# Four accumulating bias scatters moved behind the next gather, and the overflow branch moved ahead of the last rows, in a hybrid mixer and mixture-of-experts kernel

## The chip, the core and the metric

The kernel runs on one core of a Trainium2 chip. The metric is device time in microseconds (us). A lower number is better. The engines are named as the profile names them: PE (TensorE matmul), PEld (its weight load), DVE (VectorE), ACT (ScalarE), POOL (GpSimd) and SP (SyncE). A "q" behind a name (POOLq, SPq) marks work that the engine's sequencer does alone: semaphore waits, register loads, branches, drains.

## What is computed

512 tokens of width 1024 go through a normalisation, two attention-like mixers, a second normalisation and then a mixture of 32 experts of which each token takes four. The last part is where the change lies:

```python
def moe_ffn(h, w_router, b_router, w_gate_up, b_gate_up, w_down, b_down):
    logits = (xt @ w_router + b_router).astype(jnp.float32)
    top_val, top_idx = lax.top_k(logits, TOP_K)
    gates = jax.nn.softmax(top_val, axis=-1)
    ...
    def expert_block(args):
        xb, e = args
        gu = xb @ w_gate_up[e] + b_gate_up[e]
        gate = jnp.minimum(gu[:, :D_FF], SWIGLU_LIMIT)
        up = jnp.clip(gu[:, D_FF:], -SWIGLU_LIMIT, SWIGLU_LIMIT)
        glu = gate * jax.nn.sigmoid(SWIGLU_ALPHA * gate)
        return ((up + 1.0) * glu) @ w_down[e] + b_down[e]
    ys = lax.map(expert_block, (xs, blk_e)).reshape(P, D)
    ys = ys * slot_g[:, None].astype(ys.dtype)
    out = jax.ops.segment_sum(ys, slot_tok, num_segments=T)
...
h = layer_norm(DEEPNORM_ALPHA * h + ffn, ln_ffn_g[l], ln_ffn_b[l])
```

## The kernel before

Every float32 product is made of three passes over split numbers (a high and a low part, L1536 to L1538). For each weight tile ACT makes the high part (L901, `whi<-raw`), DVE subtracts it to get the low part (L1301, `wlo<-raw,whi`), and PE uses both. SP loads the tiles, 1 MB each, twelve for an expert: eight for gate and up, four for down. Six raw slots and four split slots go round; SP may load a tile as soon as DVE has split the tile six places earlier (`after`, L474).

**A step.** All five engines run a loop over i, one expert in a step. In step i PE multiplies the eight gate and up tiles of expert i, adds the bias (L1896, raises `gu_done`), transposes the gathered rows of the next expert (`turn_x`, L1543 from `xg`), multiplies the four down tiles of expert i-1, and transposes the activated rows (`turn_a`, L1543 from `act_t`). DVE splits tiles 4 to 8 of the step (counted from 0), then waits until the results of expert i-2 have been added in memory (`y_out`, ahead of L1435), copies the next row lists into `didx` and `gidx` (L1435 to L1439, raises `tab_ready`), splits tiles 9 to 11, which are the last three down tiles, and goes on to the clamps (L1377, L1379) and to the product that makes `act_t` (L1385).

**GpSimd's order.** POOL issues its DMAs in the order of the code, and a wait in it holds all that is written behind. A step of its loop (`body`, L667) is: wait for `gu_done` of this step; two small loads of the next bias (L643); the gather of rows for the expert after the next (L627), which needs `tab_ready` and the transpose `turn_x` of the rows before; then the scatter of the finished rows (`scatter`, L638), which adds `y_t` into `acc_dram` and needs ACT's `y_t` (L965) and the landing of the scatter before.

**The bias of the down product.** The gated sum of `b_down` is made once for all tokens in step 2, on PE and ACT, and lies in the tile `h2`. Four DMAs (L680), 512 KB each, add it to `acc_dram`, one for each 128 tokens, with the row numbers in `ridx`. All accumulating DMAs on `acc_dram` may not overlap those on the same rows, so the four wait for the scatter before them (`y_out`), and the next scatter waits for them (`bias_added`). The kernel before issues them behind body 2 and waits for them there, ahead of step 3 with its gather.

**The end.** After the results of 31 experts have been added, SP loads `acc_dram` in four parts, DVE normalises them, and SP stores them (`finish`, L508, L511). The rows of the last expert go another way: POOL gathers them from `acc_dram` (L691), DVE adds and normalises (L1492 to L1499, raises `last_ready`), and POOL writes them over the stored output (L697, `last_out`). An expert can have more than 128 rows; further blocks are in an overflow branch, entered if `count` (read from `ovtab`) is above zero. In these inputs it is not entered. Before, POOL takes that branch (L699) behind L697, and SP reads `count` (L519) and branches (L520) after it has waited for `last_out`. Behind its last work each engine drains and joins a barrier (L2017).

Of the kernel before, what the change touches and what calls it, by code (L numbers as in the profile page):

```python
# [13 lines left out]
ALU = mybir.AluOpType  # L14
ACT = mybir.ActivationFunctionType
F32 = mybir.dt.float32
# [8 lines left out]
T = 512  # L25
TT = T // P
# [7 lines left out]
E = 32  # L34
# [80 lines left out]
def build(nc, a, out):  # L115
    base = -(-nc.sbuf_base // 128) * 128
# [44 lines left out]
    bias_raw = at("bias_raw", 176, [P, 512])  # L161
    bias_hi = at("bias_hi", 179, [P, 512], F32R)
    bias_lo = at("bias_lo", 182, [P, 512], F32R)
# [130 lines left out]
    raw_in = [S(f"raw_in{s}") for s in range(XRAW)]  # L294
    hi_ready, lo_ready = S("hi_ready"), S("lo_ready")
    small_hi, small_lo = S("small_hi"), S("small_lo")
    bias_hi_s, bias_lo_s, bias_out = S("bias_hi_s"), S("bias_lo_s"), S("bias_out")
    h_norm, h_turned, hT_hi_s, hT_lo_s, h_out, h_back = (
        S("h_norm"), S("h_turned"), S("hT_hi_s"), S("hT_lo_s"), S("h_out"), S("h_back"))
    half_done = S("half_done")  # L300
# [41 lines left out]
    acc_in = [S(f"acc_in{t}") for t in range(TT)]  # L342
    acc_out, last_in, last_ready, last_out = S("acc_out"), S("last_in"), S("last_ready"), S("last_out")
    fin_ready, fin_out, over_done = S("fin_ready"), S("fin_out"), S("over_done")
    dve_seq, act_seq, fin_seq = S("dve_seq"), S("act_seq"), S("fin_seq")
    afin_seq = S("afin_seq")
    var_ready, std_ready, gsqrt_done = S("var_ready"), S("std_ready"), S("gsqrt_done")
# [82 lines left out]
    @block.sync  # L430
    def _(sp):
        def load_x(t):
            sp.dma_start(xt[:, t, :], x_tiles[t]).then_inc(x_in[t], 16)

        def load_params():
            w_in = a["w_in"][0].rearrange("(k p) c -> p k c", p=P)
            sp.dma_start(sm_raw[:, :, 0:RANK], w_in[:, :, C_LOW:C_LOW + RANK]).then_inc(small_in, 16)
            sp.dma_start(sm_raw[:, :, RANK:RANK + FH], w_in[:, :, C_FF:C_FF + FH]).then_inc(small_in, 16)
            sp.wait_ge(w_up_zero, 1)
            sp.dma_start(w_up[0:RANK, :], a["w_gla_gate_up"][0]).then_inc(params_in, 16)  # L440
            sp.dma_start(w_up[32:33, :], a["b_gla_gate"]).then_inc(params_in, 16)
            sp.dma_start(b_f, bcast(a["b_forget"][0], FH)).then_inc(params_in, 16)
            with nc.allow_non_contiguous_dma(reason="256 gains onto partitions"):
                sp.dma_start(g_norm, a["g_gla_norm"][0].rearrange("(c p) -> p c", p=P)).then_inc(params_in, 16)
            sp.dma_start(w_rt[:], a["w_router"][0].rearrange("(k p) e -> p k e", p=P)).then_inc(params_in, 16)
            sp.dma_start(b_rt[:], bcast(a["b_router"][0], E)).then_inc(params_in, 16)
            sp.dma_start(bias_raw[:], a["b_gate_up"][0].rearrange("e (q c) -> (e q) c", c=512)).then_inc(bias_in, 16)

        load_x(0)
        load_x(1)  # L450
        sources = {n: a[n][0] for n in ("w_in", "w_gla_proj", "w_fox_proj", "w_out")}
        for c, (kind, j, source, col) in enumerate(DENSE):
            if c >= RAW:
                o = c - RAW
                sp.wait_ge(hi_ready, o + 1)
                sp.wait_ge(lo_ready, o + 1)
            src = sources[source].rearrange("(k p) c -> p k c", p=P)[:, :, col:col + CW]
            sp.dma_start(raw[:, c % RAW, :].rearrange("p (k c) -> p k c", k=KT), src).then_inc(raw_in[c % RAW], 16)
            if c == 0:
                load_x(2)  # L460
                load_x(3)
            if c == RAW - 1:
                load_params()

        def load_gu(e, c, slot):
            sp.dma_start(xraw(slot), w_gu[e, c * P:(c + 1) * P, :]).then_inc(raw_in[slot], 16)

        def load_dn(e, q, slot):
            src = w_dn[e, 2 * q * P:2 * (q + 1) * P, :].rearrange("(p k) c -> p k c", k=2)
            sp.dma_start(xraw(slot).rearrange("p (k c) -> p k c", k=2), src).then_inc(raw_in[slot], 16)  # L470

        def after(n):

            sp.wait_ge(lo_ready, NCD + n + 1)  # L474


        sp.wait_ge(half_done, 2 * (NPROJ + 4))
        for c in range(2):
            sp.dma_start(pre[:, c, :], w_gu[0, c * P:(c + 1) * P, :]).then_inc(pre_in[c], 16)
        sp.wait_ge(wo_done, 2 * TT - 1)  # L480
        load_gu(0, 6, 0)
        load_gu(0, 7, 1)
        sp.wait_ge(wo_done, 2 * TT)
        load_gu(0, 2, 2)
        load_gu(0, 3, 3)
        sp.wait_ge(lg_done, TT)
        load_gu(0, 4, 4)
        load_gu(0, 5, 5)

        def body(i):  # L490

            for c in range(STEPC):
                after(tile_no(i, c) - XRAW)
                if c < GUC:
                    load_gu(i, c, tile_slot(c))
                else:
                    load_dn(i - 1, c - GUC, tile_slot(c))

        with sp.Fori(1, E) as i:
            body(i)  # L500
        for q in range(DNC):
            after(tile_no(E, q) - XRAW)
            load_dn(E - 1, q, tile_slot(q))

        def finish(n):

            for t in range(TT):
                sp.dma_start(acc[:, t, :], acc_tiles[t]).then_inc(acc_in[t], 16)  # L508
            for t in range(TT):
                sp.wait_ge(fin_ready, TT * n + t + 1)  # L510
                sp.dma_start(out_tiles[t], acc[:, t, :]).then_inc(fin_out, 16)  # L511
            sp.wait_ge(fin_out, 16 * TT * (n + 1))

        sp.wait_ge(y_out, 16 * (E - 1))
        finish(0)

        sp.wait_ge(last_out, 16)
        sp.wait_ge(routed, 1)
        count = sp.value_load(ovtab[0:1, 2 * OVMAX:2 * OVMAX + 1], min_val=0, max_val=OVMAX)  # L519
        with sp.If(count > 0):  # L520
            with sp.Fori(0, count) as j:
                e = sp.value_load(ovtab[0:1, bass.ds(j, 1)], min_val=0, max_val=E - 1)
                for c in range(STEPC):
                    after(NMAIN + STEPC * j + c - XRAW)
                    if c < GUC:
                        load_gu(e, c, c % XRAW)
                    else:
                        load_dn(e, c - GUC, c % XRAW)
            sp.wait_ge(over_done, 1)
            finish(1)  # L530


    @block.gpsimd
    def _(pool):
# [44 lines left out]
            pool.wait_ge(h_norm, t + 1)  # L579
            g.dma_start(h_tiles[t], xt[:, t, :]).then_inc(h_out, 16)  # L580

        pool.wait_ge(bias_hi_s, 1)
        pool.wait_ge(bias_lo_s, 1)
        for s, part in enumerate((bias_hi, bias_lo)):
            g.dma_start(bgu_dram[s].rearrange("(p c) -> p c", p=P), part[:]).then_inc(bias_out, 16)

# [77 lines left out]
        g.dma_start(lnffn_g[:], bcast(a["ln_ffn_g"][0])).then_inc(lnffn_in, 16)  # L664
        g.dma_start(lnffn_b[:], bcast(a["ln_ffn_b"][0])).then_inc(lnffn_in, 16)

        def body(i, last):  # L667
            if not last:
                pool.wait_ge(gu_done, i + 1)
                load_bgu(i + 1)  # L670
                gather(i + 3, i + 2)
            scatter(i - 1)

        body(1, False)
        body(2, False)
        pool.wait_ge(y_out, 16 * 2)
        pool.wait_ge(ridx_ready, 1)
        for t in range(TT):
            pool.wait_ge(stage_ready, TT + t + 1)
            g.indirect_dma_start(acc_dram, bass.IndirectOffsetOnAxis(ap=ridx[:, t:t + 1], axis=0), h2[:, t, :], None,  # L680
                                 bounds_check=token_bound, oob_is_err=False, compute_op=ALU.add).then_inc(bias_added, 16)
        pool.wait_ge(bias_added, 16 * TT)
        with pool.Fori(3, E - 1) as i:
            body(i, False)
        body(E - 1, True)

# [4 lines left out]
        g.indirect_dma_start(xg[:], None, acc_dram, bass.IndirectOffsetOnAxis(ap=didx[:, 0:1], axis=0),  # L691
                             bounds_check=token_bound, oob_is_err=False).then_inc(last_in, 16)
        count = pool.value_load(ovtab[0:1, 2 * OVMAX:2 * OVMAX + 1], min_val=0, max_val=OVMAX)
        pool.wait_ge(last_ready, 1)
        pool.wait_ge(fin_out, 16 * TT)
        pool.sem_inc(scatters, 1)
        g.indirect_dma_start(out[0], bass.IndirectOffsetOnAxis(ap=didx[:, 0:1], axis=0), up_t[:], None,  # L697
                             bounds_check=token_bound, oob_is_err=False).then_inc(last_out, 16)
        with pool.If(count > 0):  # L699
            pool.wait_ge(last_out, 16)  # L700
            scatter(E - 1)
            with pool.Fori(0, count) as j:
                e = pool.value_load(ovtab[0:1, bass.ds(j, 1)], min_val=0, max_val=E - 1)
                gather(E + 4 + j, E + 1 + j)
                load_bgu(e)
                scatter(E + j)


    @block.scalar
    def _(act):  # L710
# [49 lines left out]
        act.wait_ge(small_in, 32)  # L760
        s_.copy(sm_hi[:], sm_raw[:]).then_inc(small_hi, 1)
        act.wait_ge(bias_in, 16)
        s_.copy(bias_hi[:], bias_raw[:]).then_inc(bias_hi_s, 1)

        def evacuate(c, half):

# [278 lines left out]
    def _(dve):  # L1045
# [49 lines left out]
        h_lo(3)  # L1095
        dve.wait_ge(small_hi, 1)
        v.tensor_tensor(sm_lo[:], sm_raw[:], sm_hi[:].bitcast(F32), ALU.subtract).then_inc(small_lo, 1)
        dve.wait_ge(bias_hi_s, 1)
        v.tensor_tensor(bias_lo[:], bias_raw[:], bias_hi[:].bitcast(F32), ALU.subtract).then_inc(bias_lo_s, 1)

        def hook(s):
            if s == 5:
# [937 lines left out]
```

## Time and profile before

| quantity | value |
|---|---|
| median of 3 runs | 1833.65 us (1832.83 to 1834.01) |
| the profiled execution | 1832.18 us |
| its span | 1830.6 us |
| granted TensorE clock, mean | 0.987 of full speed |
| PE busy | 1765.0 us, 96% of the span |
| DVE busy | 1360.5 us, 74% |
| ACT busy | 1096.5 us, 60% |
| POOL busy | 305.3 us, 17% |
| read from HBM | 476.12 MB |

The span is the part of the profiled execution between its first and last instruction; 1.58 us lie around it. A stretch in which PE follows matmul on matmul is set by PE. Where PE waits, the row says in square brackets how long and for whom, and from there one goes back: to the engine that came late, to what that engine waited for, until an instruction is reached that nothing held. The trace's chain of work does the same from the end of the program.

### The profile page before, as it was taken

How to read it: one execution, taken by the hardware profiler on the slowest of the kernel's cores; microseconds unless marked ns; L12 is line 12 of the kernel's file. 1: busy time of each engine (PE TensorE's matmuls, PEld its weight loads, DVE VectorE, ACT ScalarE, POOL GpSimd, SP SyncE). 2: the span in 40 equal slices, each digit the busy share in tenths (PEclk: the TensorE clock that was granted, in tenths of full speed). 3: DMA queues.
4: the chain of work that ended last, by engine and by line, in shares of the span. 5: the costliest groups of instructions: out<-in, count | busy, mean ns of one | idle time of the engine just before them, and what ended most of it. 6: DMA issues, size and time to landing. Idle time of an engine off the chain costs nothing.

```text
span 1830.6 us, 24973 instructions
## 1 busy us (share of the span) xinstructions
PE 1765.0 (96%) x9025; PEld 1470.8 (80%) x9026; DVE 1360.5 (74%) x1180; ACT 1096.5 (60%) x895; POOL 305.3 (17%) x222
## 2 busy tenths in 40 slices
PE   6999999999999999999999999999999999999992
PEld 6897798888888977777888888888888888888882
DVE  6314533433346689979999999999999999999995
ACT  3522323455413257767777877777777777787772
POOL 3000000000000056231212122121221221212211
PEclk9999999999999999999999999999999999999996
DMA  7322123122233289999999999999999999999973
GB/s 255 109 75 70 47 70 92 47 70 70 92 113 138 84 328 335 379 369 379 366 368 388 364 367 389 372 367 382 377 371 379 385 367 369 391 368 367 387 301 109
DMA packets 122621, 487.51 MB, mean 266 GB/s; under 512 B 18822, under 2 KB 63878, under 8 KB 73418
## 3 DMA queue, kind: packets, MB, share of 16 engines
q1 hardware_dynamic: 106642, 455.66, 64.7%
q0 software_dynamic: 15920, 31.12, 6.1%
q8 instruction: 37, 0.61, 0.1%
q14 instruction: 14, 0.11, 0.0%
q10 hardware_dynamic: 8, 0.01, 0.0%
HBM read 476.12 MB, written 27.84 MB: 275 GB/s over the span
## 4 chain that ended last, share of the span: by engine, by line
PE 88%; DVE 4%; DMA 3%; issue 1%; ACT 1%; POOL 0%; POOLq 0%; ACTq 0%; DVEq 0%
PE psA L1536 21%; PE psA L1538 20%; PE psA L1537 20%; PE psX L1538 6%; PE psX L1537 6%; PE psX L1536 6%; PE psX L1543 3%; DMA acc_dram<-y_t,didx 2%; DMA acc_dram<-h,ridx 1%; PE psX L1706 1%; PE psX L1692 1%; PE psX L1665 1%; PE psA L1896 1%; DVE wlo L1301 1%; PE psX L1656 1%
## 5 line engine op out<-in xcount | busy, mean ns | idle before, releaser
L1301 DVE TENSOR_TENSOR wlo<-raw,whi 128x2048 fp32r<-128x2048 f32 x382 | 863.4, 2288 | 64.7 <-ACT whi L901 63.6
L901 ACT CAST whi<-raw 128x2048 fp32r<-128x2048 f32 x382 | 724.4, 1913 | 202.0 <-PE psA L1538 172.2
L1536 PE MATMUL psA<-whi,xT_hi 128*128 128x512 f32 x1020 | 400.6, 393 | 1.5 <-issue 0.9
L1537 PE MATMUL psA<-wlo,xT_hi 128*128 128x512 f32 x1020 | 397.0, 389 | 0.0
L1538 PE MATMUL psA<-whi,xT_lo 128*128 128x512 f32 x1020 | 397.0, 389 | 0.0
L1536 PEld LDWEIGHTS psA<-whi,xT_hi 128*128 128x128 f32 x1020 | 191.6, 188 | 42.1 <-issue 3.7
L1538 PEld LDWEIGHTS psA<-whi,xT_lo 128*128 128x128 f32 x1020 | 191.5, 188 | 40.0
L1537 PEld LDWEIGHTS psA<-wlo,xT_hi 128*128 128x128 f32 x1020 | 191.6, 188 | 38.4
L1536 PE MATMUL psX<-whi,aT_hi 128*128 128x512 f32 x512 | 203.8, 398 | 9.9 <-DVE aT_lo L1370 6.4
L1538 PE MATMUL psX<-whi,aT_lo 128*128 128x512 f32 x512 | 200.9, 392 | 0.0
L1537 PE MATMUL psX<-wlo,aT_hi 128*128 128x512 f32 x512 | 200.8, 392 | 0.0
L1065 DVE TENSOR_TENSOR wlo<-raw,whi 128x2048 fp32r<-128x2048 f32 x40 | 91.6, 2291 | 134.7 <-ACT whi L720 134.7
L638 POOL DMA_INDIRECT acc_dram<-y_t,didx x31 | 109.2, 3522 | 344.1 <-ACT y_t L965 321.0
L1536 PE MATMUL psA<-hT_hi,whi 128*128 128x512 f32 x416 | 165.5, 398 | 0.0
L1538 PE MATMUL psA<-hT_hi,wlo 128*128 128x512 f32 x416 | 162.4, 390 | 0.0
L1537 PE MATMUL psA<-hT_lo,whi 128*128 128x512 f32 x352 | 137.3, 390 | 0.0
L1536 PEld LDWEIGHTS psX<-whi,aT_hi 128*128 128x128 f32 x512 | 97.1, 190 | 29.8 <-issue 10.5
L643 POOL DMA_DIRECT2D bgu<-bgu_dram x64 | 38.8, 607 | 469.7 <-PE psA L1896 448.0
L1538 PEld LDWEIGHTS psX<-whi,aT_lo 128*128 128x128 f32 x512 | 97.0, 189 | 20.5
L1537 PEld LDWEIGHTS psX<-wlo,aT_hi 128*128 128x128 f32 x512 | 97.2, 190 | 19.4
L720 ACT CAST whi<-raw 128x2048 fp32r<-128x2048 f32 x40 | 76.3, 1906 | 40.6 <-PE psA L1538 40.6
L1536 PE MATMUL psA<-whi,hT_hi 128*128 128x256 f32 x320 | 95.2, 298 | 2.7 <-DVE hT_lo L1072 2.7
(350 smaller groups left out, 2309.9 us busy)
## 6 DMA issues: line engine op xcount, KB each, us to landing
raw<-in_w_gate_up SPq DMA_DIRECT2D x254, 1024.0 KB, 8.6
raw<-in_w_down SPq DMA_DIRECT2D x128, 1024.0 KB, 7.9
raw<-in_w_in SPq DMA_DIRECT2D x32, 1024.0 KB, 5.4
raw<-in_w_gla_proj SPq DMA_DIRECT2D x4, 1024.0 KB, 4.9
raw<-in_w_fox_proj SPq DMA_DIRECT2D x4, 1024.0 KB, 4.8
raw<-in_w_out SPq DMA_DIRECT2D x4, 1024.0 KB, 5.0
xt<-in_x SPq DMA_DIRECT2D x4, 512.0 KB, 6.6
h_dram<-xt POOLq DMA_DIRECT2D x4, 512.0 KB, 5.4
```

Source lines behind the costliest of these rows:

```text
L638: g.indirect_dma_start(acc_dram, bass.IndirectOffsetOnAxis(ap=didx[:, 0:1], axis=0), y_t[:], None, bounds_check=token_bound, oob_is_err=Fa ...
L643: g.dma_start(bgu[part:P:32, :], bgu_rows[part, e, :].rearrange("(n c) -> n c", c=512)).then_inc(bgu_in, 16)
L720: s_.copy(whi[:, c % SPL, :], raw[:, c % RAW, :]).then_inc(hi_ready, 1)
L901: s_.copy(xsplit(c)[0], xraw(slot)).then_inc(hi_ready, 1)
L1065: v.tensor_tensor(wlo[:, c % SPL, :], raw[:, c % RAW, :], whi[:, c % SPL, :].bitcast(F32), ALU.subtract).then_inc(lo_ready, 1)
L1301: v.tensor_tensor(lo, xraw(slot), hi.bitcast(F32), ALU.subtract).then_inc(lo_ready, 1)
L1536: mm(dst, sh, mh, start=first, stop=False)
L1537: mm(dst, sh, ml, start=False, stop=False)
L1538: return mm(dst, sl, mh, start=False, stop=last)
L1543: ins = nc.tensor.transpose(dst[:, k // 4, (k % 4) * P:(k % 4 + 1) * P], src[:, k * P:(k + 1) * P], ident[:])
L1656: ins = mm(chunk_state(n), gk[rows, n // 2, h * GDK:(h + 1) * GDK], gv[rows, n // 2, h * GDV:(h + 1) * GDV], start=True, stop=True)
L1665: ins = mm(psX[:, half, tok], state[:, n, half * P:(half + 1) * P], gq[:, h, tok], start=True, stop=True)
```

## The change

The four bias scatters become a function `add_bias`, which step 3 of POOL calls between its gather and its scatter; step 3 is written out for it ahead of the loop, which now begins with 4. In the tail POOL branches on `count` ahead of the write of the last rows and not behind it. SP reads `count` and branches ahead of its wait for `last_out`, and no longer waits for the stores of the normal path (`fin_out`) by itself. Two semaphores are merged into others with the same order of events (`bias_hi_s` into `small_hi`, `bias_lo_s` into `small_lo`). In the overflow branch, which is not entered here, POOL keeps the last write from having an effect by an `iota` on `didx`.

```diff
@@ sync
             for t in range(TT):
                 sp.wait_ge(fin_ready, TT * n + t + 1)
                 sp.dma_start(out_tiles[t], acc[:, t, :]).then_inc(fin_out, 16)
-            sp.wait_ge(fin_out, 16 * TT * (n + 1))
+            if n == 1:
+                sp.wait_ge(fin_out, 16 * TT * 2)
 
         sp.wait_ge(y_out, 16 * (E - 1))
         finish(0)
 
-        sp.wait_ge(last_out, 16)
         sp.wait_ge(routed, 1)
         count = sp.value_load(ovtab[0:1, 2 * OVMAX:2 * OVMAX + 1], min_val=0, max_val=OVMAX)
         with sp.If(count > 0):
...
             sp.wait_ge(over_done, 1)
             finish(1)
+        sp.wait_ge(last_out, 16)
@@ gpsimd
-        pool.wait_ge(bias_hi_s, 1)
-        pool.wait_ge(bias_lo_s, 1)
+        pool.wait_ge(small_hi, 2)
+        pool.wait_ge(small_lo, 2)
...
+        def add_bias():
+
+            pool.wait_ge(y_out, 16 * 2)
+            pool.wait_ge(ridx_ready, 1)
+            for t in range(TT):
+                pool.wait_ge(stage_ready, TT + t + 1)
+                g.indirect_dma_start(acc_dram, bass.IndirectOffsetOnAxis(ap=ridx[:, t:t + 1], axis=0), h2[:, t, :], None,
+                                     bounds_check=token_bound, oob_is_err=False,
+                                     compute_op=ALU.add).then_inc(bias_added, 16)
+            pool.wait_ge(bias_added, 16 * TT)
+
         def body(i, last):
             if not last:
                 pool.wait_ge(gu_done, i + 1)
                 load_bgu(i + 1)
                 gather(i + 3, i + 2)
+            if isinstance(i, int) and i == 3:
+                add_bias()
             scatter(i - 1)
 
-        body(1, False)
-        body(2, False)
-        pool.wait_ge(y_out, 16 * 2)
-        pool.wait_ge(ridx_ready, 1)
-        for t in range(TT):
-            pool.wait_ge(stage_ready, TT + t + 1)
-            g.indirect_dma_start(acc_dram, bass.IndirectOffsetOnAxis(ap=ridx[:, t:t + 1], axis=0), h2[:, t, :], None,
-                                 bounds_check=token_bound, oob_is_err=False, compute_op=ALU.add).then_inc(bias_added, 16)
-        pool.wait_ge(bias_added, 16 * TT)
-        with pool.Fori(3, E - 1) as i:
+        for i in range(1, 4):
+            body(i, False)
+        with pool.Fori(4, E - 1) as i:
             body(i, False)
         body(E - 1, True)
...
         count = pool.value_load(ovtab[0:1, 2 * OVMAX:2 * OVMAX + 1], min_val=0, max_val=OVMAX)
-        pool.wait_ge(last_ready, 1)
-        pool.wait_ge(fin_out, 16 * TT)
-        pool.sem_inc(scatters, 1)
-        g.indirect_dma_start(out[0], bass.IndirectOffsetOnAxis(ap=didx[:, 0:1], axis=0), up_t[:], None,
-                             bounds_check=token_bound, oob_is_err=False).then_inc(last_out, 16)
         with pool.If(count > 0):
-            pool.wait_ge(last_out, 16)
+            pool.wait_ge(last_ready, 1)
+            pool.wait_ge(fin_out, 16 * TT)
             scatter(E - 1)
...
+            pool.wait_ge(over_done, 1)
+            g.iota(didx[:], [[0, 1]], base=T, channel_multiplier=0).then_inc(none_left, 1)
+            pool.wait_ge(none_left, 1)
+        pool.wait_ge(last_ready, 1)
+        pool.wait_ge(fin_out, 16 * TT)
+        pool.sem_inc(scatters, 1)
+        g.indirect_dma_start(out[0], bass.IndirectOffsetOnAxis(ap=didx[:, 0:1], axis=0), up_t[:], None,
+                             bounds_check=token_bound, oob_is_err=False).then_inc(last_out, 16)
```

POOL's instructions of steps 2 and 3 before. `bgu` are the bias loads, `xg` the gathered rows, `h_89` is the tile `h2`; the rows from the first branch on are the loop, whose first pass is step 3:

```order
L627 DMA xg<-h_dram,gidx 128x1024 [waits tab_ready,xt_done]
L638 DMA acc_dram<-y_t,didx 512x1024 [waits y_ready,y_out]
L680 DMA acc_dram<-h_89,ridx 512x1024 [waits stage_ready,ridx_ready,y_out]
L680 DMA acc_dram<-h_89,ridx 512x1024 [waits stage_ready] x3
L683 UNCONDITIONAL_BRANCH [waits bias_added]
L683 ISA
L643 ISA [waits gu_done]
L643 DMA bgu<-bgu_dram 4x512
L643 ISA
L643 DMA bgu<-bgu_dram 4x512
L624 REGISTER_ALU
L625 REGISTER_ALU [waits tab_ready]
```

The same place with the change, from step 2's gather on:

```order
L629 DMA xg<-h_dram,gidx 128x1024 [waits tab_ready,xt_done]
L640 DMA acc_dram<-y_t,didx 512x1024 [waits y_ready,y_out]
L645 DMA bgu<-bgu_dram 4x512 [waits gu_done]
L645 DMA bgu<-bgu_dram 4x512
L629 DMA xg<-h_dram,gidx 128x1024 [waits tab_ready,xt_done]
L675 DMA acc_dram<-h_89,ridx 512x1024 [waits stage_ready,ridx_ready,y_out]
L675 DMA acc_dram<-h_89,ridx 512x1024 [waits stage_ready] x3
L640 DMA acc_dram<-y_t,didx 512x1024 [waits y_out,bias_added,y_ready]
```

The wait for `gu_done`, two bias loads and a gather now stand ahead of the four bias scatters, and nothing but a wait stands between these and the scatter of `y_t`.

POOL's end before, with the write of the last rows and then the branch:

```order
L691 DMA xg<-acc_dram,didx 128x1024 [waits xt_done,tab_ready,y_out]
L693 TENSOR_LOAD ovtab
L693 ISA x2
L697 DMA out_h<-up_t,didx 512x1024 [waits last_ready,fin_out]
L699 COMPARE_AND_BRANCH
```

POOL's end with the change. The rows between, left out, are the overflow branch:

```order
L699 DMA xg<-acc_dram,didx 128x1024 [waits xt_done,tab_ready,y_out]
L701 TENSOR_LOAD ovtab
L701 ISA x2
L702 COMPARE_AND_BRANCH
...
L702 UNCONDITIONAL_BRANCH [waits none_left]
L717 DMA out_h<-up_t,didx 512x1024 [waits last_ready,fin_out]
```

The branch has moved ahead of the last write.

## Rows read from the trace of the kernel before

**Rows 1.** The page: busy time, and the chain that ended last by engine

```profile
PE 1765.0 (96%) x9025; PEld 1470.8 (80%) x9026; DVE 1360.5 (74%) x1180; ACT 1096.5 (60%) x895; POOL 305.3 (17%) x222
...
PE 88%; DVE 4%; DMA 3%; issue 1%; ACT 1%; POOL 0%; POOLq 0%; ACTq 0%; DVEq 0%
```

**Rows 2.** Timeline of PE, `turn_x` of four steps: start, duration, line, shape

```profile
747.66 1.09 PE L1543 MATMUL psX<-ident,xg 128*128 128x128 f32 x8
...
782.68 0.55 PE L1543 MATMUL psX<-ident,xg 128*128 128x128 f32 x3
...
817.73 0.87 PE L1543 MATMUL psX<-ident,xg 128*128 128x128 f32 x6
...
860.21 0.98 PE L1543 MATMUL psX<-ident,xg 128*128 128x128 f32 x7
```

**Rows 3.** Timeline of PE in step 4; brackets: idle before, and who ended it

```profile
825.10 0.76 PE L1536 MATMUL psX<-whi,aT_hi 128*128 128x512 f32 x1 [3.53 <-DVE wlo L1301]
825.66 0.63 PE L1537 MATMUL psX<-wlo,aT_hi 128*128 128x512 f32 x1
...
828.57 0.39 PE L1538 MATMUL psX<-whi,aT_lo 128*128 128x512 f32 x1
...
836.97 1.09 PE L1543 MATMUL psX<-ident,act_t 128*128 128x128 f32 x8 [1.85 <-DVE act_t L1385]
```

**Rows 4.** Timeline of DVE in step 4

```profile
822.05 0.15 DVE L1435 COPY didx<-lrows 128x1 uint32 x1 [5.60 <-DMA acc_dram<-y_t,didx]
...
822.66 6.70 DVE L1301 TENSOR_TENSOR wlo<-raw,whi 128x2048 fp32r<-128x2048 f32 x3
...
835.62 1.22 DVE L1385 SCALAR_TENSOR_TENSOR act_t<-up_t,act_t 128x1024 f32<-128x1024 f32 x1
```

**Rows 5.** Timeline of POOL, steps 2 and 3

```profile
748.04 1.24 POOL L643 DMA_DIRECT2D bgu<-bgu_dram  x2 [18.14 <-PE psA L1896]
749.59 3.01 POOL L627 DMA_INDIRECT xg<-h_dram,gidx  x1 [0.30 <-issue]
...
776.44 3.43 POOL L680 DMA_INDIRECT acc_dram<-h,ridx  x1 [9.22 <-DMA acc_dram<-y_t,didx]
...
785.61 2.41 POOL L680 DMA_INDIRECT acc_dram<-h,ridx  x1 [0.30 <-issue]
805.83 1.23 POOL L643 DMA_DIRECT2D bgu<-bgu_dram  x2 [17.82 <-DMA acc_dram<-h,ridx]
...
810.07 2.76 POOL L638 DMA_INDIRECT acc_dram<-y_t,didx  x1 [0.30 <-issue]
```

**Rows 6.** Writers of `acc_dram`, 776 to 830 us: the bias scatters, and landing

```profile
L680 POOL DMA_INDIRECT acc_dram<-h,ridx x4: 2401/2412/3430, 776.4 to 785.6; - x4
...
DMA to landing us min/median/max: 11.9/14.8/19.4
```

**Rows 7.** All 31 scatters of `y_t` (line L638): from issue to landing

```profile
L638 POOL DMA_INDIRECT acc_dram<-y_t,didx x31: 2055/3657/3693, 727.4 to 1786.6; - x31
...
DMA to landing us min/median/max: 8.3/12.6/13.6
```

**Rows 8.** DMA queues in 776 to 805 us: packets, MB, share of 16 engines

```profile
q1 hardware_dynamic: 1095, 7.99, 66.9%
q0 software_dynamic: 576, 2.10, 36.2%
```

**Rows 9.** Timeline of POOL from 1818 us: the last write

```profile
1818.85 1.02 POOL L697 DMA_INDIRECT out_h<-up_t,didx  x1 [21.52 <-issue]
```

**Rows 10.** The drains and the branches of the tail: min/median/max ns, start us

```profile
L2017 POOLq DRAIN  x1: 11532/11532/11532, 1818.8 to 1818.8; - x1
L2017 SPq DRAIN  x1: 53/53/53, 1823.5 to 1823.5; - x1
...
L699 POOLq COMPARE_BRANCH  x1: 53/53/53, 1818.6 to 1818.6; - x1
...
L2002 PEldq COMPARE_BRANCH  x1: 4571/4571/4571, 1799.9 to 1799.9; - x1
```

More of the change, by code:

```diff
@@ L296, in build @@
     small_hi, small_lo = S("small_hi"), S("small_lo")
-    bias_hi_s, bias_lo_s, bias_out = S("bias_hi_s"), S("bias_lo_s"), S("bias_out")
+    bias_out = S("bias_out")
     h_norm, h_turned, hT_hi_s, hT_lo_s, h_out, h_back = (
@@ L344, in build @@
     fin_ready, fin_out, over_done = S("fin_ready"), S("fin_out"), S("over_done")
+    none_left = S("none_left")
     dve_seq, act_seq, fin_seq = S("dve_seq"), S("act_seq"), S("fin_seq")
@@ L762, in _ @@
         act.wait_ge(bias_in, 16)
-        s_.copy(bias_hi[:], bias_raw[:]).then_inc(bias_hi_s, 1)
+        s_.copy(bias_hi[:], bias_raw[:]).then_inc(small_hi, 1)
         def evacuate(c, half):
@@ L1097, in _ @@
         v.tensor_tensor(sm_lo[:], sm_raw[:], sm_hi[:].bitcast(F32), ALU.subtract).then_inc(small_lo, 1)
-        dve.wait_ge(bias_hi_s, 1)
-        v.tensor_tensor(bias_lo[:], bias_raw[:], bias_hi[:].bitcast(F32), ALU.subtract).then_inc(bias_lo_s, 1)
+        dve.wait_ge(small_hi, 2)
+        v.tensor_tensor(bias_lo[:], bias_raw[:], bias_hi[:].bitcast(F32), ALU.subtract).then_inc(small_lo, 1)
         def hook(s):
```

## The prediction

> **What bounds the kernel now.** I read the busy table first: PE is busy for 96% of the span, and the chain that ended last lies on PE for 88% of it [rows 1]. Whatever delays PE delays the end, and a change that touches only GpSimd and SyncE counts only where PE waits for something that hangs on their DMAs, or in the tail, where PE is done. The second view is PE's timeline, read at one instruction that comes once in a step: `turn_x` starts at 747.66, 782.68, 817.73 and 860.21 us [rows 2]. The steps last 35.02, 35.05 and 42.48 us. So one step, number 4 (it begins at about 795 and its `turn_x` is the one at 817.73), costs about 7.5 us more than its neighbours in what follows that `turn_x`. This is the only place in the expert loop near the moved scatters where time is lost, and it is what the change acts on.
>
> The third view follows the loss back. PE stood 3.53 us until 825.10, for `wlo`, which DVE made late [rows 3]. Behind that wait PE's matmuls take 0.63 us each in the record and not 0.39 until about 828.5 [rows 3], and PE waits once more, 1.85 us until 836.97, for `act_t`. DVE had stood 5.60 us until 822.05, at the copy of `didx`, for the scatter of `y_t` (expert 2's rows) to land in `acc_dram` [rows 4]. From there DVE works through: three tiles (6.70 us), the clamps, and `act_t` from 835.62 [rows 4]. PE's second wait ends at 836.97, 14.92 us behind the copy at 822.05. That distance is DVE and ACT work in a fixed row. So the whole loss of 7.5 us hangs on one moment: when the scatter of `y_t` has landed. If it lands X us later, PE loses X us more; PE's slower matmuls lie inside that distance, with 1.85 us to spare.
>
> POOL's timeline says why it lands at 822 [rows 5]: the scatter of step 2 has landed at 776.4, the four bias scatters are issued from 776.44 to 785.61, POOL waits 17.82 us for the last of them until 805.83, then issues step 3's two bias loads and its gather, and only at 810.07 the scatter of `y_t`. It lands 11.9 us behind its issue [rows 6], at 822.0.
>
> **The change, part by part.**
>
> *The bias scatters behind the gather of step 3.* They can't be issued before `gu_done` of step 3, two bias loads and a gather. In step 2 the bias loads begin 0.38 us behind the start of `turn_x` (748.04 against 747.66), the gather begins 1.55 us later and lasts 3.01 us on POOL [rows 2, 5]; the next DMA follows 0.30 us behind. That is 5.24 us behind `turn_x`. With step 3's `turn_x` at 782.68, the first bias scatter goes out at 787.92 and not at 776.44: 11.48 us later.
>
> From its first issue to the last landing the block takes 785.61 - 776.44 + 19.4 = 28.57 us [rows 5, 6], so now it ends at 816.49 and not at 805.01. Then the scatter of `y_t` follows at once: 0.3 us instead of the 5.06 us from 805.01 to 810.07 [rows 5]. It is issued at 816.8, lands 11.9 us later [rows 6], at 828.7, and not at 822.0. So X = 11.48 - 4.76 = 6.7 us. The gather that is moved ahead gains nothing: its rows were in use at 817.73 in time [rows 2], and no row shows PE waiting for `xg`. What is queued behind the waiting POOL is the scatter of `y_t` first, then the next bias loads, which PE needs 35 us later; who waits for the scatter is DVE, with the last three down tiles behind it, and PE for those.
>
> The unknown is how long the DMAs take in the new place. Both ends: the scatter of `y_t` landed in 8.3 to 13.6 us over the whole run [rows 7], so -3.6 or +1.7 against 11.9. POOL's issue of the gather is 2.4 us in the loop against my 3.01, so -0.6, and the release can take the 0.8 us that the row of 805.83 shows, so +0.5. The gather is now in flight beside the bias scatters. A scatter's share of the block is 28.57 / 4 = 7.1 us, which is an upper price for one more transfer of its size; it starts 3.3 us ahead, so +3.8 at most. The ends of X are then 2.5 and 12.7 us. I keep 6.7, since each term is from the row of the same kind nearest in time, and the traffic beside them (12 tiles a step from SP) is the same in either place: in 776 to 805 us the weights took 66.9% of the DMA engines' time and the software queue 36.2% [rows 8].
>
> A page speaks against these durations. The trace shows 19.4 us for the last bias scatter and never under 8.3 us for a scatter of `y_t` [rows 6, 7]. The Trainium skill, DMA: Bandwidth & Descriptors, section on the anatomy of one DMA, fits a GpSimd DMA by about 2.0 us plus its bytes over 436 GB/s, which by its figures is an estimate of 3.2 us for one of these. By that rule DVE's wait would vanish and the kernel would be faster by the 7.5 us; the rows disagree, since here the transfers accumulate and share the engines with the weight loads.
>
> *The tail.* DVE's last instruction releases POOL, which issues the last write at 818.85 [rows 9]. Its sequencer's branch behind it lasts 53 ns [rows 10] and the drain begins at 818.79, before the write itself starts on POOL. So the branch is no part of the way to the write, and moved ahead it lies in the 21.52 us in which POOL waits [rows 9]. Its worth is 0 to 0.2 us. SP reads `count` and branches behind `last_out`, and its drain is at 1823.5, while POOL's drain, begun at 1818.79, lasts 11.53 us, to 1830.3 [rows 10]. SP is done some 6.8 us ahead of the end, so what it saves is hidden by POOL's drain. What that drain waits for, no row says; it stays behind the write in both orders, so I price it unchanged. I take -0.1 us for the tail.
>
> *The merged semaphores* keep the same order of events 1800 us ahead of the end; the step of POOL that is written out removes a loop pass. Nothing waits for either: 0.
>
> **Sum.** Against the profiled execution of 1832.18 us (span 1830.6 and 1.58 around it): +6.7 - 0.1 gives 1838.8. The median of the runs is 1.5 us above that execution, 1833.65, so the forecast is 1840.2 us.
>
> **The rivals.**
>
> *Faster: the scatters are only slow where they stand now.* If in the new place each transfer lands like the fastest of [rows 7], 8.3 us, the block ends 9.17 + 8.3 us behind its first issue, at 805.4, and the scatter of `y_t` at 814.0. DVE comes to its wait at 816.45 (822.05 less 5.60) and doesn't stop; the 7.5 us come back: 1826.1 us. It decides by one number: from the first bias issue to the landing of `y_t` there are 34.1 us (787.9 to 822.0) before the kernel is slower, and 28.5 before DVE waits at all; now it would be 40.8. For it: the weight loads are a moving load, and POOL issues four in 9 us. Against it: the four share the queues with the same traffic as before.
>
> *The tail gives more than its branch.* The nearest dear branch is PE's, 4.57 us [rows 10], against 0.05 for POOL's. The Trainium skill, Runtime: NRT & Kernel Launch, section on instruction fetch mechanics, has a taken branch out of the fetched window stall for a fetch. If a stall of that kind sits within POOL's drain and the branch takes it along, the tail is shorter by 4.6 us (PE's row), or by up to 8.1 if the drain then ends with the last landing at about 1822.2. With +6.7 that gives 1835.8 to 1832.3 us: within the 0.2% of no change. Against it: the drain is in the trace right behind the branch [rows 10], so its code was there.
>
> *Little traffic.* X of 2.5 to 3.6 us, with a landing near 8.3 us for `y_t` alone because SP's loads run dry while DVE stands: 1836.0 to 1837.2, also within 0.2%.
>
> *Worse contention.* The gather in front costs its full share and weight tiles come late too: X above 10 us, 1844 to 1848.
>
> That the change doesn't do what it says is excluded: the listing of POOL's instructions shows the gather ahead of the scatters.
>
> **How the numbers follow.** About 0.2% (3.7 us) is what a measurement of this kernel can tell from no change. Forecast (X of 3.7 to 10): 0.70. Worse contention: 0.08, also slower. Little traffic 0.06 and the tail 0.08: no change. Faster by the scatters: 0.08. So faster 0.08, same 0.14, slower 0.78. The range runs from 1836.0 (X of 2.5) to 1846.0 (X of 12.5, the contention priced nearly in full); it leaves out the faster case, the tail's, and the end of contention, 0.19 together.
>
> **What the profile of the changed kernel would show.** Four bias scatters from about 787.9 us, the last landing near 816.5; the scatter of `y_t` from about 816.8; DVE's wait at the copy of `didx` near 12 us instead of 5.60, PE's wait for `wlo` near 10 instead of 3.53; the next `turn_x` at about 867 and not 860.21; steps of 35.0 us behind it; in the tail the same drain of some 11.5 us on POOL, and SP done earlier. I am wrong if the bias block is much shorter than 28.6 us, if PE waits somewhere else in steps 3 to 5, or if POOL's drain changes its length.

## The result, and the profile after

The changed kernel takes 1837.80 us in the median of 13 runs (1835.89 to 1841.02), the kernel before 1833.48 us beside it (13 runs, 1832.83 to 1834.63). The ratio is 1.0024, with a 95% interval of 1.0017 to 1.0031: slower by 4.3 us. The prediction said 1840.2, with 1836.0 to 1846.0 around it.

The profiled execution took 1837.37 us (span 1835.8), 5.19 us more than the one of before. PE's timeline, read at `turn_x` as in [rows 2] (the code has moved, so line L1543 of before is now L1555), shows where:

```profile
748.52 1.09 PE L1555 MATMUL psX<-ident,xg 128*128 128x128 f32 x8
...
783.55 1.09 PE L1555 MATMUL psX<-ident,xg 128*128 128x128 f32 x8
...
818.57 1.09 PE L1555 MATMUL psX<-ident,xg 128*128 128x128 f32 x8
...
865.37 1.09 PE L1555 MATMUL psX<-ident,xg 128*128 128x128 f32 x8
```

The steps are 35.03, 35.02 and 46.80 us; in the kernel before the last of the three was 42.48. That step alone is 4.3 us longer. Another 0.86 us arose ahead of the changed place (`turn_x` at 748.52 against 747.66) and 0.06 us in the tail; the medians' difference of 4.3 us has the size of that step alone.

POOL's timeline from step 3 on (columns: start, duration, line, tile out and in, idle time before with its releaser) answers to [rows 5]:

```profile
783.93 1.21 POOL L645 DMA_DIRECT2D bgu<-bgu_dram  x2 [15.85 <-PE psA L1908]
785.46 2.95 POOL L629 DMA_INDIRECT xg<-h_dram,gidx  x1 [0.31 <-issue]
788.71 1.65 POOL L675 DMA_INDIRECT acc_dram<-h,ridx  x1 [0.30 <-issue]
...
795.54 3.03 POOL L675 DMA_INDIRECT acc_dram<-h,ridx  x1 [0.30 <-issue]
815.50 3.09 POOL L640 DMA_INDIRECT acc_dram<-y_t,didx  x1 [16.93 <-DMA acc_dram<-h,ridx]
```

The gather now stands ahead of the four bias scatters, POOL waits 16.93 us for the last of these to land, and the scatter of `y_t` goes out at 815.50 instead of 810.07. Two rows on landing, the first of the writers of `acc_dram` from 780 to 830 us (min, median, max; it answers to [rows 6]), the second of the DMA issues from 783 to 818 us (the last column is the landing time of the `y_t` scatter):

```profile
DMA to landing us min/median/max: 10.1/13.4/19.2
```

```profile
acc_dram<-y_t,didx POOLq DMA_INDIRECT x1, 11.6
```

The block ends at 795.54 + 19.2 = 814.7, and `y_t` lands at 815.50 + 11.6 = 827.1. DVE's and PE's timelines, which answer to [rows 4] and [rows 3]:

```profile
827.18 0.15 DVE L1447 COPY didx<-lrows 128x1 uint32 x1 [10.01 <-DMA acc_dram<-y_t,didx]
```

```profile
830.23 0.77 PE L1548 MATMUL psX<-whi,aT_hi 128*128 128x512 f32 x1 [7.82 <-DVE wlo L1313]
...
842.11 1.09 PE L1555 MATMUL psX<-ident,act_t 128*128 128x128 f32 x8 [1.21 <-DVE act_t L1397]
```

DVE waits 10.01 us instead of 5.60, PE 7.82 instead of 3.53; the second wait of PE is 1.21 us. From DVE's copy to PE's `act_t` it is 842.11 - 827.18 = 14.93 us; in before it was 836.97 - 822.05 = 14.92. PE alone in three stretches of the step (busy us with count, granted clock as a share of 2.4 GHz, DMA share, GB/s):

```profile
818.50:831.00 12.50, 4.68 (x26) 0.75 0.72 281
831.00:842.00 11.00, 9.90 (x35) 0.82 0.83 314
842.00:850.00 8.00, 7.89 (x39) 1.00 0.92 337
```

While PE stands, the granted clock leaves its upper level (2.4 GHz) and is back there in the third stretch. The lower clock lies inside the 14.9 us that DVE needs anyway, and costs nothing of its own here.

In the tail, POOL's last write and its drain (second fence: sequencer rows, min/median/max in ns, start) answer to [rows 9] and [rows 10]:

```profile
1824.06 1.02 POOL L717 DMA_INDIRECT out_h<-up_t,didx  x1 [21.67 <-issue]
```

```profile
L2029 POOLq DRAIN  x1: 11364/11364/11364, 1824.2 to 1824.2; - x1
...
L2029 SPq DRAIN  x1: 13/13/13, 1827.5 to 1827.5; - x1
```

From the last `turn_x` to the end of the span it is 59.80 us, against 59.74 in before. The reordered tail changes nothing.

### The profile page after: what moved, and what is told of

Same layout as the page of the kernel before. It is cut to its first block, busy times and chain, and to the rows that moved or that the text cites. A ratio compares the mean times of both kernels' runs of the same rounds, so it can differ in the third digit from the quotient of the medians.

```text
span 1835.8 us, 24964 instructions
## 1 busy us (share of the span) xinstructions
PE 1767.6 (96%) x9025; PEld 1472.8 (80%) x9026; DVE 1361.0 (74%) x1180; ACT 1096.4 (60%) x895; POOL 294.4 (16%) x222
## 4 chain that ended last, share of the span: by engine, by line
PE 90%; DVE 4%; DMA 3%; ACT 1%; issue 1%; POOL 0%; ACTq 0%; DVEq 0%; POOLq 0%
PE psA L1548 21%; PE psA L1549 21%; PE psA L1550 21%; PE psX L1550 6%; PE psX L1549 6%; PE psX L1548 6%; PE psX L1555 3%; DMA acc_dram<-y_t,didx 1%; DMA acc_dram<-h,ridx 1%; PE psX L1718 1%; PE psX L1704 1%; PE psX L1677 1%; PE psA L1908 1%; PE psX L1668 1%; DVE orstd L1153 1%
```

## The experiments

**Each part alone.** The first kernel has only the moved scatters, the second only the tail and the merged semaphores.

```diff
-        body(1, False)
-        body(2, False)
-        pool.wait_ge(y_out, 16 * 2)
...
+            if isinstance(i, int) and i == 3:
+                add_bias()
             scatter(i - 1)
```

> The bias scatters alone are moved, as in the change; tail and semaphores stay as before. Theory (the loss follows the landing of the scatter of y_t in step 3): all of the changed kernel's +4.3 us is here, so +3.8 to +5.0 against the kernel before; the step behind turn_x 4 lasts 46 to 47 us and not 42.5. Rival (part of the loss is in the tail or in the merged semaphores): +1 to +3 us.

Measured: 1838.24 us, before beside it 1834.23, ratio 1.0022 (1.0013 to 1.0031), so +4.0 us as the theory had it. The step behind `turn_x` 4 takes 47.23 us.

```diff
         with pool.If(count > 0):
-            pool.wait_ge(last_out, 16)
+            pool.wait_ge(last_ready, 1)
+            pool.wait_ge(fin_out, 16 * TT)
...
+        g.indirect_dma_start(out[0], bass.IndirectOffsetOnAxis(ap=didx[:, 0:1], axis=0), up_t[:], None,
```

> The tail and the merged semaphores of the change, with the bias scatters where they stood before. Theory (GpSimd's drain stays behind the last write, some 10.5 us behind the end of its instruction): -0.3 to +0.2 us, the drain again some 11.4 us, SyncE's drain earlier but still ahead of GpSimd's. Rival (the branch moved ahead of the write is paid or won): -1 us or more, or +1 us or more.

Measured: 1834.07 us, ratio 0.9995 (0.9986 to 1.0004). The moved scatters carry the whole loss, the tail none.

This profiled execution, with the scatters in their old place, shows something else as well. Its step behind `turn_x` 3 takes 35.94 us and the next one 43.60, so 9.5 us are lost where the one of before lost 7.5. Yet DVE waited only 2.23 us at the copy, and its third tile behind it waited for ACT:

```profile
820.30 0.15 DVE L1441 COPY didx<-lrows 128x1 uint32 x1 [2.23 <-DMA acc_dram<-y_t,didx]
...
826.27 2.29 DVE L1307 TENSOR_TENSOR wlo<-raw,whi 128x2048 fp32r<-128x2048 f32 x1 [0.40 <-ACT whi L907]
```

So the landing of `y_t` was not what decided there. The next experiments show what did.

**The wait moved and not the scatters.** Here the four bias scatters stay in their old place, and only the wait for their landing goes behind the gather, right ahead of the scatter of `y_t`. POOL then doesn't hold back the bias loads and the gather.

```diff
+            if added:
+                pool.wait_ge(bias_added, 16 * added)
             scatter(i - 1)
...
-        pool.wait_ge(bias_added, 16 * TT)
-        with pool.Fori(3, E - 1) as i:
+        bias_tiles(0, 4, 2)
+        body(3, False, 4)
+        with pool.Fori(4, E - 1) as i:
```

> The four bias scatters are issued where they stood before, but the wait for them stands right ahead of the scatter of y_t in step 3, behind the bias loads and the gather. Theory: the scatter of y_t goes out about 4.8 us sooner (at 805.3 and not at 810.1), less what the gather beside the four takes from them (0 to 3.3 us), so -1.5 to -4.8 us. Rival (the 2 MB that the four move beside the weight loads cost the time, wherever the waits stand): -0.5 to +0.5 us.

Measured: 1834.19 us, ratio 1.0001 (0.9992 to 1.001). The scatter of `y_t` did land some 5 us earlier (issued at 806.05, landing in 11.1 us), and DVE's timeline has no bracket at the copy, so DVE didn't wait:

```profile
821.42 0.15 DVE L1442 COPY didx<-lrows 128x1 uint32 x1
```

The theory's 1.5 to 4.8 us did not come back; the rival's range held. Two steps lost 8.1 us together (37.07 and 41.07 instead of 35.02). PE's timeline still has the second wait, and the table of waits in 783 to 830 us (total, times, longest) tells who was late instead:

```profile
836.72 1.52 PE L1550 MATMUL psX<-ident,act_t 128*128 128x128 f32 x8 [3.90 <-DVE act_t L1392]
```

```profile
ACT whi L908 <- DMA raw<-in_w_gate_up: 8.1, 5, 2.7
ACT whi L908 <- DMA raw<-in_w_down: 4.6, 4, 2.8
```

The first column of numbers is the total: ACT, which makes `whi` of every weight tile, waited 12.7 us for tiles that SP loads. A second limit lies behind the one that the prediction found, and at almost the same size.

**The bias scatters left out.** The result lacks the bias term; everything else is done.

```diff
-        pool.wait_ge(y_out, 16 * 2)
-        pool.wait_ge(ridx_ready, 1)
-        for t in range(TT):
...
-        pool.wait_ge(bias_added, 16 * TT)
         with pool.Fori(3, E - 1) as i:
```

> The four bias scatters are left out (the gated sum of b_down is never added), with their waits; all else as before. It gives the most that any place of them can be worth. Theory: DVE's wait of 5.60 us, PE's two waits and its slower matmuls are gone, -7.0 to -7.6 us. If less than 6 us come back, something else in this stretch held PE too. It doesn't tell waits and traffic apart; the run with the late wait and those with the scatters spread over steps do.

Measured: 1825.60 us, before beside it 1834.23, ratio 0.9954 (0.994 to 0.9967); from `turn_x` 2 (748.25 us) on every step is 35.02 or 35.03 us. The median is 8.6 us lower, more than the 7.0 to 7.6 expected; part of that is that the profiled execution of before, with its 7.5 us, is faster than any of the 13 runs timed beside the changed kernel, and two others with the scatters in the old place lost more here (9.5 us with the tail only, 7.8 in the run without the last write). The same stretch, 783 to 818 us, in this kernel and in the one with the late wait: first the two queues (packets, MB, share of 16 engines), then the weight loads (count, KB, median landing). No bias:

```profile
q1 hardware_dynamic: 1722, 12.54, 90.9%
q0 software_dynamic: 352, 0.43, 5.1%
...
raw<-in_w_gate_up SPq DMA_DIRECT2D x8, 1024.0 KB, 9.4
raw<-in_w_down SPq DMA_DIRECT2D x4, 1024.0 KB, 9.0
```

Late wait:

```profile
q1 hardware_dynamic: 1349, 9.83, 68.2%
q0 software_dynamic: 928, 2.53, 35.1%
...
raw<-in_w_gate_up SPq DMA_DIRECT2D x6, 1024.0 KB, 17.8
raw<-in_w_down SPq DMA_DIRECT2D x4, 1024.0 KB, 15.0
```

A plain step keeps the DMA engines busy for 96% of its time. The scatters bring 2.1 MB, whose packets take 30% of 35 us, 10.5 us of all 16 engines. (The shares of the two queues then add up to 103%, so the packets' times overlap a little, and 10.5 us is an upper value of what the scatters take from the weight loads.) The weight loads fall from 12.54 to 9.83 MB in the stretch and land in 15 to 18 us instead of 9.

**Traffic without a wait.** To see the second limit alone, the four scatters keep their place but add into the tensor `h_dram`, which nobody reads any more, and nobody waits for them until three steps later. (The gathers read another tensor, `h2_dram`; the views leave buffer numbers out and print both as `h_dram`.) The result lacks the bias term.

```diff
-            g.indirect_dma_start(acc_dram, bass.IndirectOffsetOnAxis(ap=ridx[:, t:t + 1], axis=0), h2[:, t, :], None,
+            g.indirect_dma_start(h_dram, bass.IndirectOffsetOnAxis(ap=ridx[:, t:t + 1], axis=0), h2[:, t, :], None,
...
+        for i in range(3, 6):
+            body(i, False)
         pool.wait_ge(bias_added, 16 * TT)
```

> The four scatters are issued where they stood before, but add into h_dram, which nobody reads any more, and nothing waits for them until step 6 (the bias is left out of the result). So the scatter of y_t in step 3 goes out in time, near 799 us, and the same 2 MB pass beside the weight loads. Theory of two limits (the late landing of y_t and late weight tiles, each of which alone would hold PE in this stretch; the later one counts): the step behind turn_x 4 still lasts 41 to 43 us, by ACT's waits for down tiles, so -1.5 to +0.5 us against the kernel before. Theory of the landing alone: 35.0 us, -7 to -8.6 us.

Measured: 1833.31 us, ratio 0.9995 (0.9986 to 1.0004). The scatter of `y_t` goes out at 801.43, and DVE waits for nothing at the copy; still the two steps are 39.13 and 38.85 us, 7.9 us lost. The table of waits in 783 to 830 us:

```profile
ACT whi L903 <- DMA raw<-in_w_gate_up: 10.3, 5, 2.9
```

The traffic alone, with no wait on POOL, costs as much as the kernel before loses; the theory of the landing alone, which had 35.0 us for these steps, is out.

**A late landing without the traffic.** The opposite: no bias scatters (their term is missing in the result), but the scatter of step 3's `y_t` is held back until the fifth expert's first half is done.

```diff
+            if isinstance(i, int) and i == 3:
+                pool.wait_ge(gu_done, 5)
             scatter(i - 1)
```

> No bias scatters (left out of the result), and the scatter of y_t in step 3 is held by a wait until gu_done 5, that is until about turn_x 4. A late landing without the traffic. In the kernels before and changed the loss of the step behind turn_x 4 was the landing, counted from turn_x 4, plus 3.3 us (4.2 and 7.5; 8.5 and 11.8). By that law, with an issue 0.7 us behind turn_x 4 and a landing 11 to 12.6 us later, the step loses 15 to 16.6 us: 50 to 51.6 us long, and +6.4 to +8.2 us against the kernel before in all. If the loss needed the traffic too, it stays under 12 us.

Measured: 1835.83 us, ratio 1.0009 (1.0 to 1.0018); against the 1825.60 without bias, from another set of runs, this is 10.2 us. Timelines of POOL, DVE and PE, and the landing of this one scatter:

```profile
822.26 1.65 POOL L638 DMA_INDIRECT acc_dram<-y_t,didx  x1 [31.10 <-PE psA L1892]
```

```profile
828.38 0.15 DVE L1431 COPY didx<-lrows 128x1 uint32 x1 [11.30 <-DMA acc_dram<-y_t,didx]
```

```profile
831.43 0.77 PE L1532 MATMUL psX<-whi,aT_hi 128*128 128x512 f32 x1 [6.26 <-DVE wlo L1297]
...
843.32 1.09 PE L1539 MATMUL psX<-ident,act_t 128*128 128x128 f32 x8 [2.07 <-DVE act_t L1381]
```

```profile
DMA to landing us min/median/max: 6.0/6.0/6.0
```

The expectation of mine was too high, since I took a landing of 11 to 12.6 us, and with few weight loads in flight it was 6.0. The chain is the predicted one: copy to `act_t` 843.32 - 828.38 = 14.94 us. (The profiled execution is this kernel's longest, 1840.69 us; 2 to 3 us of that lie ahead of the first `turn_x`, which comes at 677.8 us and in the other runs' profiles at 674.8 to 675.8.)

**The scatters spread over steps.** If the bunched traffic costs 8 us, it should cost less apart. The first two of these runs were forecast by the landing alone, the last two by two limits. Two behind step 2 and two behind step 3; one behind each of steps 2 to 5; one behind steps 2, 4, 6, 8; one behind steps 2, 5, 8, 11. The wait stands ahead of the next scatter of `y_t`.

```diff
+        bias_tiles(0, 2, 2)
+        body(3, False, 2)
+        bias_tiles(2, 2, 3)
+        body(4, False, 4)
```

> Two of the four bias scatters are issued behind the scatter of step 2, two behind that of step 3, and each pair is waited for right ahead of the next scatter of y_t. The same 2 MB move in the same way. Theory: in a step GpSimd's accumulating queue is free from about 776 to 799 us, and two scatters land 18 us behind the first issue, so no scatter of y_t comes late: -7.0 to -7.6 us, as without any bias scatter. Rival (traffic costs the time): it is the same in sum, so between -2 and +1 us.

Measured: 1832.11 us, before 1833.83, ratio 0.9984 (0.9976 to 0.9993). That is -1.7 us and not the theory's -7.0 to -7.6; the rival, the traffic, was right. One step lost 6.7 us, again with no wait of DVE for `y_t`; ACT's timeline at the last down tile, and PE's behind it:

```profile
821.93 1.91 ACT L910 CAST whi<-raw 128x2048 fp32r<-128x2048 f32 x1 [3.10 <-DMA raw<-in_w_down]
```

```profile
833.78 1.96 PE L1552 MATMUL psX<-ident,act_t 128*128 128x128 f32 x8 [3.61 <-DVE act_t L1394]
```

```diff
+        bias_tiles(0, 1, 2)
+        body(3, False, 1)
+        bias_tiles(1, 1, 3)
+        body(4, False, 2)
...
```

> As the run with two and two, with one bias scatter behind each of the steps 2 to 5. Theory: also -7.0 to -7.6 us, no better than two and two, since none is late there already. Rival (traffic): each step has a quarter of it; better than two and two by 1 us or more if weight tiles still come late there.

Measured: 1829.63 us, ratio 0.9975 (0.9963 to 0.9986). The theory fell here too (-4.2 us), and the rival was right again: 2.5 us better than two and two. The steps stay at 35.0 us until about the fourth scatter, then lose 2.0 us. (The profiled execution, 1827.85 us, is this kernel's fastest; the median is 1.8 us above it.)

```diff
+        bias_tiles(0, 1, 2)
+        body(3, False, 1)
+        body(4, False)
+        bias_tiles(1, 1, 4)
+        body(5, False, 2)
...
```

> One bias scatter behind each of the steps 2, 4, 6 and 8. Theory of two limits, with the DMA engines 96 to 97% busy in a plain step: a scatter puts the weight loads back by some 2.5 us, a plain step wins back about 1.2 us, and one a step left 2.0 us lost at the fourth. With every other step free the debt never reaches PE: all steps 35.0 us, -7.3 to -8.6 us, as without any bias scatter, and 2 us or more below one in each step. If the scatters cost by themselves it is no better than one in each step (-4.2 us).

Measured: 1826.04 us, before 1833.74, ratio 0.9958 (0.9944 to 0.9971): -7.7 us, and every step is 35.0 us, as the theory of two limits had it.

```diff
+        bias_tiles(0, 1, 2)
+        body(3, False, 1)
+        body(4, False)
+        body(5, False)
+        bias_tiles(1, 1, 5)
...
```

> One bias scatter behind each of the steps 2, 5, 8 and 11. Theory of two limits: the same as with every other step, within 0.5 us, since nothing is left to win. If each scatter leaves more debt than two steps win back, this is faster than the run with every other step by 1 us or more.

Measured: 1825.63 us, ratio 0.9954 (0.994 to 0.9967), the same as with no bias scatter at all. It is the whole computation, 8.1 us faster than the kernel before (1833.74 beside it) and about 12 us faster than the changed one. Two of its bias scatters on POOL's timeline, and the landing of all four:

```profile
777.28 3.06 POOL L673 DMA_INDIRECT acc_dram<-h,ridx  x1 [9.59 <-DMA acc_dram<-y_t,didx]
...
882.70 2.72 POOL L673 DMA_INDIRECT acc_dram<-h,ridx  x1 [9.97 <-DMA acc_dram<-y_t,didx]
```

```profile
DMA to landing us min/median/max: 11.7/12.0/12.5
```

One scatter more raises the software queue's share of a 35 us stretch (783 to 818 us) from the 5.1% without bias to:

```profile
q0 software_dynamic: 496, 0.96, 12.6%
```

That is 7.5% of 35 us, 2.6 us of all engines for one, and a plain step leaves 4% of its time, 1.4 us. My reading, worked out and not shown by itself: one scatter in two or three steps (2.6 us against 2.8 or more left over) fits in; one in each step is short by 1.2 us a step and has used up by the fourth what the loads are ahead; and four at once overrun both, by the 8 us measured.

**The drain.** The last write of POOL is left out, and with it the last rows of the result.

```diff
-        pool.sem_inc(scatters, 1)
-        g.indirect_dma_start(out[0], bass.IndirectOffsetOnAxis(ap=didx[:, 0:1], axis=0), up_t[:], None,
-                             bounds_check=token_bound, oob_is_err=False).then_inc(last_out, 16)
+        pool.sem_inc(last_out, 16)
```

> The write of the last expert's rows (the last DMA of GpSimd) is left out of the kernel before; its waits stay, and its semaphore is raised by GpSimd's sequencer. It measures what stands behind DVE's last instruction. Theory (GpSimd's drain ends a fixed 10.5 us behind the end of its last DMA instruction): that instruction is now the gather at 1796.3, the drain is short, and the end is set by the other engines' branches, at 1819 to 1821: -9.5 to -11.5 us. Rival (the drain has a length of its own whatever stood ahead of it): the drain is again 10 to 11.5 us long and the end moves by no more than 1 us.

Measured: 1831.99 us, ratio 0.9986 (0.9978 to 0.9995). POOL's last DMA on its timeline and its drain:

```profile
1797.22 1.06 POOL L691 DMA_INDIRECT xg<-acc_dram,didx  x1 [6.15 <-DVE small L1467]
```

```profile
L2015 POOLq DRAIN  x1: 10522/10522/10522, 1819.5 to 1819.5; - x1
```

No DMA of POOL is younger than 22 us when the drain begins, and it lasts 10.5 us all the same. My theory that it waits for the last write fell. With the write the drain is 11.36 us in the changed kernel and 11.53 in [rows 10], and ends 10.45 us behind the write instruction in both. So of the tail the write costs its own 1.0 us, and the rest is the drain's. What it does in that time stays open.

## Why the prediction was right, and where it was only half right

**The place and the mechanism.** The prediction said that everything hangs on the landing of `y_t`, that X us later there is X us more for PE, and that the tail is worth nothing. For this change it held. DVE's copy came 822.05 - 817.73 = 4.32 us behind `turn_x` in before and 827.18 - 818.57 = 8.61 us behind it now: 4.29 us later, and the step is 4.31 us longer. An undisturbed step has `act_t` 11.85 us behind `turn_x` (830.15 against 818.30 with no bias), and the fixed row from the copy is 14.93 us, so the loss of a step should be the copy's distance plus 3.08 us. That gives 7.40 for before (measured 7.46), 11.69 for after (11.78), and 10.13 with the late landing (`turn_x` at 821.33; measured 11.84). The rest of the last one lies behind the second wait: from `act_t` to the next `turn_x` it is 24.9 us there and 23.3 in after, with a granted clock of 0.76 in 843 to 850 us there and 1.00 in 842 to 850 in after.

**The terms.** The first bias scatter was put 5.24 us behind `turn_x`; it came at 788.71 - 783.55 = 5.16. The landing of `y_t` was put at 11.9 us; it was 11.6. The mis-sized term is the block of 28.57 us: it took 814.74 - 788.71 = 26.03, since from POOL's first issue to its fourth it was 6.83 us and not 9.17, while the last landing was as forecast (19.2 against 19.4). From its end to the next issue it was 0.76 us and not 0.3. So X was 4.3 us and not 6.7. The range had allowed for it (its lower end was an X of 2.5), for other reasons: I had bounded the landings and the gather, and not the issue time of the scatters themselves, though [rows 6] show 2.4 to 3.4 us for one and [rows 7] 2.1 to 3.7. Of the signs of being wrong that the prediction named, the block's length came nearest: 2.5 us under its 28.6. The median was to lie 1.5 us above the profiled execution; it lies 0.4 above. (In the passage on the tail, 818.85 and 818.79 stand for 1818.85 and 1818.79.)

**What was half right.** "The whole loss of 7.5 us hangs on one moment" is true for a later landing only. With the landing 5 us earlier, the loss was 8.1 us and not 2.5 (late wait), and with no wait at all 7.9 us (traffic alone). In before two limits met at the same place: the landing of `y_t`, and the down tiles, for which ACT waited as well. Its timeline in before, one row of the last cast:

```profile
823.66 1.90 ACT L901 CAST whi<-raw 128x2048 fp32r<-128x2048 f32 x1 [2.20 <-DMA raw<-in_w_down]
```

That tile was late by the traffic and not by DVE's wait: SP issued its load at 808.97 us, ahead of that wait, and it landed 14.6 us later. Its cast ends at 823.66 + 1.90 = 825.56, while DVE came to it, the third of its three tiles [rows 4], at about 827.1. So an estimate from these rows gives an earlier landing at most 1.5 us, after which ACT is the one that PE and DVE wait for.

I had read PE's wait to DVE and DVE's to the scatter, and stopped there. The step that fails is "if it lands X us later, PE loses X us more" read backwards: the rival "faster" priced a quick landing at 1826.1 us on that ground. The late wait had its landing 5 us earlier and gave nothing back. The time that the rival named can be had, but by spreading the traffic. That the forecast held is in part luck of direction: this change moved the landing later, the one way in which the landing alone decides.

**The tail.** Worth 0, as forecast, and for the reason given: POOL's drain ends 6.8 us behind SP's in before (1830.3 against 1823.5) and 8.0 behind it now (1835.5 against 1827.5), and the branch was never on the way to the write.

**The page weighed.** The lowest landing that any run here shows for a scatter of `y_t` is 6.0 us, with few weight loads beside it; 11.6 in the changed kernel. The Trainium skill, DMA: Bandwidth & Descriptors, section on the anatomy of one DMA, would by its figures give an estimate of 3.2 us. The measurements decide against it for these transfers. The prediction gave two reasons, that they accumulate and that they share the engines with the weight loads; the step from 11.6 to 6.0 us goes with fewer loads, but no run moved the same bytes without adding them, so the first stays untested.

## What to carry to other kernels

When PE stands for one late transfer, look for the next limit before pricing an earlier landing: push the transfer out of the way in an experiment, and see whether the loss goes. Where weight loads keep the DMA engines busy for 96% of a step, an extra burst costs about its own transfer time less what is left over, even if nothing waits for it (here up to 10.5 us less 1.4; 7.9 measured); cut it into pieces two or three steps apart, which here gave back all 8 us. Moving such a burst later behind other work, with the next scatter queued behind its landing, made the wait longer here, by 4.3 us.

## What the hardware showed that I had not expected

- Bytes through the accumulating scatters are dear by the time of their packets: 0.53 MB took 2.6 us of all 16 DMA engines, 0.2 MB per us, while the weight loads moved 12.54 MB in 90.9% of 35 us, 0.39 MB per us.
- POOL's issue of one such scatter took 1.6 to 3.8 us for the same shape, and from the first to the fourth in a row it was 6.8 us in the new place and 9.2 in the old.
- POOL's drain at the end of the block lasts 10.5 us even when its last DMA is 22 us old.
